# A routed MoE step on one core: the second tile's root, the last bias products and the first block's opening moved within the routing

## The chip, the cores and the metric

The kernel runs on one core of one Trainium2 chip. The metric is the device time of one execution in microseconds (us). The median of three executions stands against the median of the changed kernel. One further execution was profiled.

## The reference, cut to what matters

One trunk layer over 528 prompt rows and 8 sample rows (536 tokens, width 1024): a mixer (diagonal state space and gated convolution), an output projection, and a mixture of experts. Around the change this is computed:

```python
x  = x + mix @ w_out                                  # residual after the mixer
hf = rmsnorm(x, norm_ffn)                             # input of router and experts
logits = hf @ w_router + b_router                     # 32 experts
top_v, top_i = lax.top_k(logits, 4)
gates = softmax(top_v)
# tokens are sorted by expert and laid into blocks of 128 rows, one expert each
gu = xe @ w_gate_up[e] + b_gate_up[e]                 # 1024 -> 2048
gate, up = min(gu[:, :1024], 7), clip(gu[:, 1024:], -7, 7)
h = gate * sigmoid(1.702 * gate) * (up + 1)
y = h @ w_down[e] + b_down[e]                         # 1024 -> 1024
x = x + sum over the 4 experts of gates * y
out = rmsnorm(x, norm_final)
```

All arrays are float32.

## The kernel before, in words

Three stages share one core, each a block of code of its own with a barrier between them: `mixer`, `router` and `experts`. The change lies in `router` (line 1042 on) and in the opening of `experts` (line 1596 on). Each stage writes out one instruction order for each engine by hand: PE (TensorE, matmuls), DVE (VectorE), ACT (ScalarE), POOL (GpSimd) and SP (SyncE, which issues most DMAs). Semaphores join them; `a.wait_ge(s, n)` holds an engine until the count is there, and everything behind it on that engine with it.

**Router.** The 536 tokens are five tiles, worked in the order `TILES` = 4, 0, 1, 2, 3 (the first holds 24 rows). The number q counts them in that order, and Q = 4 is the last. For each tile PE projects the mixer's output (`project`, L1294), DVE adds it to x (`residual`, L1460 and L1462), ACT squares (`square`), DVE forms the variance (L1468), ACT takes the root by a logarithm and an exponential (`root`, L1187 and L1189), and DVE refines it and writes hf (`normed`, L1416 to L1480). PE transposes x (L1307), ACT copies it out (`take_xT`, L1197), and PE computes the logits (`strips` L1322, `logits` L1328). DVE picks four experts (`pick_experts`, L1488 to L1501), ACT exponentiates (`expo`) and spreads the gates (`spread`, L1225), and DVE forms the gates and splits each in three bf16 parts (`gates`, L1517 to L1528). PE counts ranks (L1334, L1338) and DVE takes them (`take_ranks`, L1511 and L1512).

After the last tile, block 0 of the expert loop is prepared. DVE writes one-hot rows, PE selects the tokens of expert 0 (L1378), DVE makes the index `idx_next`, and POOL gathers those rows of hf from DRAM (L1178). Meanwhile PE computes the gate-weighted b_down rows: ten products, two for each tile (`bias_rows`, L1346). Product j takes the strip of 32 array rows number j % 4 and writes a PSUM bank of the list `BD_BANK`. ACT copies each out (`take_bias`, L1230). The tables for overflow blocks (`overflow_tables` on DVE) need counts (L1383), a prefix sum (L1391) and two limit products (L1394, L1395) of PE. At the end PE transposes the gathered rows (L1400). ACT makes the high half of weight unit 0 and of x (`w_hi` L1270, `x_hi` L1273), and DVE makes the low halves (`w_lo` L1550, `x_lo` L1555).

**Experts.** One block per expert, 32 and one overflow block. A block has 24 weight units. ACT makes a unit's high half (L1753), DVE its low half (L1925), and PE multiplies hi x hi, hi x lo and lo x hi (`products`, L1856, six matmuls a unit). The next block's selection (`select`, L1834) comes ahead of unit 8, its gather after it, and its transpositions (L1841) and bias rows (`set_bias`, L1863, four matmuls of K = 3 that open the banks) ahead of unit 20. Only block 0 has its selection and bias rows outside the loop, behind the barrier.

Of the kernel before, what the change touches and what calls it, by code (L numbers as in the profile page):

```python
# [19 lines left out]
ALU = mybir.AluOpType  # L20
ACT = mybir.ActivationFunctionType
AX_X = mybir.AxisListType.X

P = 128
# [16 lines left out]
E = 32  # L41
# [1000 lines left out]
def router(nc, a, scratch, stack, sb, sem, bank, keep, mid, tb):  # L1042

    def buf(name, shape, dt=F32):
# [48 lines left out]
        "sub exp mask rank_psum ranked acc_set gates gate4 bdn_in gT_psum gT bd_psum step act_step pool_step tabs first_psum xg_clear "  # L1093
        "count_psum extra upto_psum passed over_psum".split())}
    hf_stored = [sem("r_hf_stored0"), sem("r_hf_stored1")]
    keep["landed"] = [sem(f"landed{j}") for j in range(LOADS)]
    keep["loop"] = {n: sem("e_" + n) for n in "onehot idx x_in xT_psum x_hi x_lo w_hi w_lo".split()}
    e = keep["loop"]
# [5 lines left out]
    keep["tiles"] = TILES  # L1104
    BD_BANK = [1, 2, 3, 4, 5, 0, 1, 2, 4, 5]
    BD_AFTER = {6: 1, 7: 2, 8: 4, 9: 5}
    RT = 1.0 / math.sqrt(D)
# [74 lines left out]
    def _(act):  # L1182
# [57 lines left out]
        square(1, 1)  # L1240
        take_strips(0)
        expo(0)
        spread(0)
        root(1)
        for q in range(2, NT):
# [20 lines left out]
        nc.scalar.activation(gT[:, Q * P:NT * P], bank[3][:, 0:P], ACT.Copy).then_inc(s["gT"], 1)  # L1266
        for j in range(5, 2 * NT):
            take_bias(j)
        act.wait_ge(keep["landed"][0], 16)
        nc.scalar.activation(tb["w_hi0"][:, 0, :].rearrange("p (u n) -> p u n", u=2), unit0, ACT.Copy).then_inc(e["w_hi"], 1)  # L1270
        for h in range(2):
            act.wait_ge(*((s["gT_psum"], 3), (e["xT_psum"], 1))[h])
            nc.scalar.activation(tb["x_hi"][:, 4 * h:4 * h + 4, :].rearrange("p k t -> p (k t)"), bank[h][:], ACT.Copy).then_inc(e["x_hi"], 1)  # L1273

    @block.tensor
    def _(pe):
# [96 lines left out]
        for j in range(4):  # L1373
            bias_rows(j)
        ranks(Q)
        pe.wait_ge(e["onehot"], 1)
        for i in range(NT):
            last = nc.tensor.matmul(bank[6][:, 200:203], onehot[:, i, :], tb["slotval"][:, i, 0, 0, :], start=(i == 0), stop=(i == NT - 1))  # L1378
        last.then_inc(s["first_psum"], 1)
        for j in range(4, 2 * Q):  # L1380
            bias_rows(j)
        for j in range(NT):
            last = nc.tensor.matmul(bank[7][0:E, NT * E:NT * E + 1], mask_b[:, j, :], ones_b[:, 0:1], start=(j == 0), stop=(j == NT - 1))  # L1383
        last.then_inc(s["count_psum"], 1)
        pe.wait_ge(s["gate4"], NT)
        pe.wait_ge(keep["bd_sb"], 3)
        nc.tensor.transpose(bank[3][:, 0:P], gate4[:, Q].rearrange("p c e -> p (c e)"), ident[:]).then_inc(s["gT_psum"], 1)
        pe.wait_ge(s["gT"], 2)
        bias_rows(2 * Q)
        pe.wait_ge(s["extra"], 1)  # L1390
        nc.tensor.matmul(bank[7][0:E, NT * E + 1:NT * E + 2], tri[0:E, 0:E], extra_b[:], start=True, stop=True).then_inc(s["upto_psum"], 1)  # L1391
        bias_rows(2 * Q + 1)
        pe.wait_ge(s["passed"], 1)
        nc.tensor.matmul(bank[6][:, 256:256 + NB], ones_b[0:E, :], passed[:], start=True, stop=True)  # L1394
        nc.tensor.matmul(bank[6][:, 256 + NB:256 + 2 * NB], extra_b[:].to_broadcast([E, P]), passed[:], start=True, stop=True).then_inc(s["over_psum"], 1)  # L1395
        pe.wait_ge(e["x_in"], 16)
        pe.wait_ge(keep["bd_sb"], 7)
        for h in range(2):
            for k in range(4 * h, 4 * h + 4):
                last = nc.tensor.transpose(bank[h][:, (k % 4) * P:(k % 4 + 1) * P], xg[:, k * P:(k + 1) * P], ident[:])  # L1400
            last.then_inc(s["gT_psum"] if h == 0 else e["xT_psum"], 1)

    @block.vector
    def _(dve):
# [109 lines left out]
        def gates(q):  # L1514
            i = TILES[q]
            dve.wait_ge(s["exp"], q + 1)
            done(v.tensor_tensor(gate[:, i, :], gate[:, i, :], mask_b[:, i, :], ALU.mult))  # L1517
            done(v.tensor_reduce(gsum[:, i:i + 1], gate[:, i, :], AX_X, ALU.add))
            done(v.tensor_scalar(gsum[:, i:i + 1], gsum[:, i:i + 1], 1e-30, None, ALU.max))
            done(v.reciprocal(gsum[:, i:i + 1], gsum[:, i:i + 1]))  # L1520
            v.tensor_scalar(gate[:, i, :], gate[:, i, :], gsum[:, i:i + 1], None, ALU.mult).then_inc(s["gates"], 1)
            dve.wait_ge(s["gates"], q + 1)
            left = gate
            for c in range(3):
                part = slotval[:, i, :, 1, c]
                done(v.tensor_copy(part, left[:, i, :]))
                if c < 2:
                    done(v.tensor_tensor(rest[:, i, :], left[:, i, :], part, ALU.subtract))  # L1528
                    left = rest

        def overflow_tables():

            nth = tb["iota_s"]
            dve.wait_ge(s["count_psum"], 1)
            done(v.tensor_copy(count[:], bank[7][0:E, NT * E:NT * E + 1]))
            done(v.tensor_scalar(tiles_in[:], nth[0:E, 1:NT], float(P), count[:, 0:1], ALU.mult, ALU.is_lt))
            done(v.tensor_reduce(extra[:], tiles_in[:], AX_X, ALU.add))
            v.tensor_copy(extra_b[:], extra[:]).then_inc(s["extra"], 1)
            dve.wait_ge(s["upto_psum"], 1)
            done(v.tensor_tensor(upto[:], bank[7][0:E, NT * E + 1:NT * E + 2], extra[:], ALU.add))  # L1540
            v.tensor_scalar(passed[:], nth[0:E, 0:NB], upto[:, 0:1], -0.5, ALU.subtract, ALU.is_gt).then_inc(s["passed"], 1)
            dve.wait_ge(s["over_psum"], 1)
            ended, before = bank[6][:, 256:256 + NB], bank[6][:, 256 + NB:256 + 2 * NB]
# [8 lines left out]
            for h in range(2):  # L1552
                dve.wait_ge(e["x_hi"], h + 1)
                c = slice(4 * h, 4 * h + 4)
                last = v.tensor_tensor(tb["x_lo"][:, c, :].rearrange("p k t -> p (k t)"), bank[h][:],  # L1555
                                       tb["x_hi"][:, c, :].rearrange("p k t -> p (k t)").bitcast(F32), ALU.subtract)
# [10 lines left out]
        residual(1, 1)  # L1567
        normed(0)
        pick_experts(0)
        gates(0)  # L1570
        take_ranks(0)
        variance(1)
        normed(1)
        for q in range(2, NT):
            residual(q, 0)
            pick_experts(q - 1)
            gates(q - 1)
            take_ranks(q - 1)
            residual(q, 1)
# [16 lines left out]
def experts(nc, a, out, scratch, stack, sb, sem, bank, keep, mid, tb, landed):  # L1596
# [33 lines left out]
    def total(q):  # L1630
# [3 lines left out]
    s = {n: sem("e_" + n) for n in (  # L1634
        "w_used sel_psum sel bias_used clip sig h hT_psum h_hi h_lo "
        "y_sb y_stored y_out y_free curd turns".split())}
# [192 lines left out]
    def _(pe):  # L1829
# [60 lines left out]

        select(0, 0)
        pe.wait_ge(s["x_lo"], 1)
        set_bias(0)
        with pe.Fori(0, E - 1) as e:
# [6 lines left out]
    def _(dve):  # L1901
# [73 lines left out]
        dve.wait_ge(s["sel_psum"], 1)  # L1975
        v.tensor_reduce(sel[:], bank[7][:, 0:6].rearrange("p (a c) -> p a c", a=2), AX_X, ALU.add).then_inc(s["sel"], 1)
        for j in range(1, SLOTS):
# [66 lines left out]
```

## Time and profile before

| quantity | us |
|---|---|
| median of 3 executions (1466.55 to 1467.43) | 1466.92 |
| the profiled execution | 1467.44 |
| its span, from first to last instruction | 1465.5 |
| PE busy | 1419.3 |
| DVE busy | 1320.9 |
| ACT busy | 1031.1 |

The span is counted from the first instruction. Busy time is the time in which an engine ran its own instructions; it overlaps from engine to engine. In the rows further down, L1346 is line 1346 of the kernel, and PEld is the weight load of TensorE, which overlaps its matmuls.

### The profile page before, as it was taken

Reading aid. Unit: us, or ns where it says so; the run is one execution under the profiler, and the core shown is the slowest. Engines: PE = TensorE matmul, PEld = TensorE weight load, DVE = VectorE, ACT = ScalarE, POOL = GpSimd, SP = SyncE. Lnnn points to the kernel's source line nnn. Section 1 sums busy time; section 2 is a strip of 40 time slices with the busy share of each in tenths; the row PEclk is TensorE's granted clock in tenths of the full one; section 3 lists DMA queues with packets and bytes.
Section 4 is the critical chain, followed back from the end, with each engine's and each line's share of the span. In section 5 each row is a group of like instructions: output and inputs, shape, how many; then the busy total and the mean of one; then the engine's idle time right before and its main releaser. Section 6 shows DMA issues by size and latency. Waiting matters only on the chain.

```text
span 1465.5 us, 22683 instructions
## 1 busy us (share of the span) xinstructions
PE 1419.3 (97%) x7043; PEld 1134.9 (77%) x7044; DVE 1320.9 (90%) x1755; ACT 1031.1 (70%) x1244; POOL 142.1 (10%) x151
## 2 busy tenths in 40 slices
PE   6999999899999999999999999999999999999992
PEld 5888844588888888888888888888888888888882
DVE  4887576899999999999999999999999999999994
ACT  4011432788878888888888888888888887888783
POOL 8100020100000000000000001000000010000000
PEclk9999999799999999999999999999999999999996
DMA  9510572799999999999999999998999999999953
GB/s 308 70 34 1 197 281 115 239 403 383 381 382 375 376 377 368 373 373 376 370 373 374 371 375 375 362 357 356 366 378 375 382 382 372 370 375 372 371 223 122
DMA packets 85286, 469.42 MB, mean 320 GB/s; under 512 B 17935, under 2 KB 19207, under 8 KB 68361
## 3 DMA queue, kind: packets, MB, share of 16 engines
q1 hardware_dynamic: 73160, 447.86, 76.3%
q0 software_dynamic: 12096, 21.18, 6.3%
q8 instruction: 17, 0.28, 0.1%
q14 instruction: 13, 0.10, 0.0%
HBM read 457.56 MB, written 27.82 MB: 331 GB/s over the span
## 4 chain that ended last, share of the span: by engine, by line
PE 80%; DMA 1%; DVE 1%; ACT 0%; issue 0%; SPq 0%; POOLq 0%
PE bank L1856 75%; PE bank L1847 2%; PE bank L1841 2%; PE bank L1863 1%; DMA token_sums<-ymix,row_cur 0%; DMA x<-token_sums 0%; PE bank L1834 0%; DVE x L2006 0%; DVE ymix L2006 0%; ACT ymix L1791 0%; ACT ring_lo L1815 0%; SPq L1692 0%; DVE ssf L71 0%; DVE ssf L69 0%; DVE ssf L68 0%
## 5 line engine op out<-in xcount | busy, mean ns | idle before, releaser
L1925 DVE TENSOR_TENSOR w_lo<-ring_lo,w_hi 128x1024 fp32r<-128x1024 f32 x527 | 610.0, 1220 | 22.5 <-ACT w_hi L1753 22.4
L1753 ACT ACTIVATE w_hi<-ring_lo 128x1024 fp32r<-128x1024 f32 x527 | 544.2, 1058 | 84.9 <-PE bank L1856 80.7
L1856 PE MATMUL bank<-w_hi,x_hi 128*128 128x512 f32 x1056 | 332.7, 396 | 0.0
L1856 PE MATMUL bank<-w_lo,x_hi 128*128 128x512 f32 x1056 | 326.6, 391 | 0.0
L1856 PE MATMUL bank<-w_hi,x_lo 128*128 128x512 f32 x1056 | 326.4, 390 | 0.0
L1925 DVE TENSOR_TENSOR w_lo<-w_out,w_hi 128x1024 fp32r<-128x1024 f32 x264 | 311.2, 1221 | 11.8 <-ACT w_hi L1753 11.8
L1753 ACT ACTIVATE w_hi<-w_out 128x1024 fp32r<-128x1024 f32 x264 | 268.3, 1055 | 18.5 <-PE bank L1856 18.5
L1856 PEld LDWEIGHTS bank<-w_lo,x_hi 128*128 128x128 f32 x1056 | 198.9, 188 | 42.1
L1856 PEld LDWEIGHTS bank<-w_hi,x_lo 128*128 128x128 f32 x1056 | 198.8, 188 | 42.0
L1856 PEld LDWEIGHTS bank<-w_hi,x_hi 128*128 128x128 f32 x1056 | 194.0, 189 | 37.0 <-issue 0.4
L1856 PE MATMUL bank<-w_hi,h_hi 128*128 128x512 f32 x528 | 169.9, 403 | 0.0
L1856 PE MATMUL bank<-w_lo,h_hi 128*128 128x512 f32 x528 | 163.6, 391 | 0.0
L1856 PE MATMUL bank<-w_hi,h_lo 128*128 128x512 f32 x528 | 162.9, 390 | 0.0
L1721 POOL DMA_INDIRECT token_sums<-ymix,row_cur x33 | 52.3, 1585 | 740.3 <-ACT ymix L1791 740.3
L1856 PEld LDWEIGHTS bank<-w_lo,h_hi 128*128 128x128 f32 x528 | 99.1, 188 | 21.8
L1856 PEld LDWEIGHTS bank<-w_hi,h_lo 128*128 128x128 f32 x528 | 99.1, 188 | 21.7
L1856 PEld LDWEIGHTS bank<-w_hi,h_hi 128*128 128x128 f32 x528 | 94.1, 188 | 22.9 <-issue 7.2
L1764 ACT ACTIVATE cmix<-bank 128x512 f32<-128x512 f32 x66 | 39.6, 600 | 64.4 <-PE bank L1856 64.4
L530 PE MATMUL bank<-hT,ring_lo 128*128 128x272 f32 x240 | 74.6, 392 | 0.0
L529 PE MATMUL bank<-hT,ring_lo 128*128 128x264 f32 x240 | 73.6, 388 | 0.0
L1768 ACT ACTIVATE h_hi<-bank 128x512 fp32r<-128x512 f32 x66 | 39.5, 599 | 46.1 <-PE bank L1847 46.1
L1714 POOL DMA_INDIRECT ymix<-ffn_in,idx_next x33 | 38.9, 1178 | 334.8 <-DVE idx_next L1914 334.8
(365 smaller groups left out, 1175.4 us busy)
## 6 DMA issues: line engine op xcount, KB each, us to landing
ring_lo<-in_w_gate_up SPq DMA_DIRECT2D x132, 2048.0 KB, 11.7
w_out<-in_w_down SPq DMA_DIRECT2D x132, 1024.0 KB, 13.9
ring_lo<-in_w_in SPq DMA_DIRECT2D x4, 2048.0 KB, 22.2
w_out<-in_w_out SPq DMA_DIRECT2D x2, 2048.0 KB, 9.0
x<-in_x_prompt SPq DMA_DIRECT2D x6, 512.0 KB, 9.7
bias<-bias_rows SPq DMA_DIRECT2D x132, 3.0 KB
token_sums<-x SPq DMA_DIRECT2D x4, 512.0 KB
ffn_in<-hf SPq DMA_DIRECT2D x4, 512.0 KB, 6.6
```

The lines of the kernel that those rows point to most:

```text
L529: nc.tensor.matmul(lo[:, 0:HALF], w_k(ORDER[n], k), hT[:, k, 0:HALF], start=(k == 0), stop=(k == KD - 1))
L530: last = nc.tensor.matmul(hi[:, 0:REST], w_k(ORDER[n], k), hT[:, k, HALF:TOK], start=(k == 0), stop=(k == KD - 1))
L1714: nc.gpsimd.indirect_dma_start(xg, None, scratch["hf"], bass.IndirectOffsetOnAxis(ap=idx_next[:, 0:1].bitcast(U32), axis=0), bounds_check= ...
L1721: nc.gpsimd.indirect_dma_start(scratch["acc"], bass.IndirectOffsetOnAxis(ap=row_cur[:, 0:1].bitcast(U32), axis=0), yo, None, bounds_check= ...
L1753: nc.scalar.activation(high(j), raw(j), ACT.Copy).then_inc(s["w_hi"], 1)
L1764: nc.scalar.activation(g_sb, bank[2 * half][:], ACT.Gelu_apprx_sigmoid).then_inc(s["sig"], 1)
L1768: nc.scalar.activation(h_hi[:, 4 * half:4 * half + 4, :].rearrange("p k t -> p (k t)"), bank[6 + half][:], ACT.Copy).then_inc(s["h_hi"], 1)
L1841: last = nc.tensor.transpose(bank[6 + k // 4][:, (k % 4) * P:(k % 4 + 1) * P], xg[:, k * P:(k + 1) * P], ident[:])
L1847: last = nc.tensor.transpose(bank[6 + half][:, k * P:(k + 1) * P], h_sb[:, k * P:(k + 1) * P], ident[:])
L1856: last = nc.tensor.matmul(bank[b + u][:], v[:, k, :], part(j)[:, u, :], start=(j == 16 and first), stop=(j in (7, 15, UNITS - 1) and part ...
L1863: last = nc.tensor.matmul(bank[b][:], tb["one_b"][32 * c:32 * c + 3, 0:1].to_broadcast([3, P]), tb["bias"][32 * c:32 * c + 3, :], start=Tr ...
L1925: v.tensor_tensor(low(j), raw(j), high(j).bitcast(F32), ALU.subtract).then_inc(s["w_lo"], 1)
```

## The change

1. In the router, tile q = 1 has its variance (DVE) placed behind `normed(0)` and its root (ACT) ahead of `expo(0)`. The split of gates is a function of its own, `gate_parts`.
2. Bias product 8 goes to bank 3, and products 8 and 9 are issued side by side. The counts go to bank 6 and are taken before the one-hot rows; the prefix sum comes before the two products. For the last tile, `gate_parts` comes behind the overflow counts.
3. ACT converts weight unit 0 before it copies out bias products 8 and 9.
4. Block 0's selection (to bank 6) and its bias rows are computed in the router, and its transpositions go to banks 4 and 7.

```diff
@@ semaphores, banks
-        "count_psum extra upto_psum passed over_psum".split())}
+        "count_psum extra upto_psum passed".split())}
-    keep["loop"] = {n: sem("e_" + n) for n in "onehot idx x_in xT_psum x_hi x_lo w_hi w_lo".split()}
+    keep["loop"] = {n: sem("e_" + n) for n in "onehot idx x_in xT_psum x_hi x_lo w_hi w_lo sel_psum bias_used".split()}
-    BD_BANK = [1, 2, 3, 4, 5, 0, 1, 2, 4, 5]
-    BD_AFTER = {6: 1, 7: 2, 8: 4, 9: 5}
+    BD_BANK = [1, 2, 3, 4, 5, 0, 1, 2, 3, 5]
+    BD_AFTER = {6: 1, 7: 2, 9: 5}
+    XT_BANK = (4, 7)
@@ router, scalar
         take_strips(0)
+        root(1)
         expo(0)
         spread(0)
-        root(1)
...
-        for j in range(5, 2 * NT):
+        for j in range(5, 2 * Q):
             take_bias(j)
         act.wait_ge(keep["landed"][0], 16)
         nc.scalar.activation(tb["w_hi0"]..., unit0, ACT.Copy).then_inc(e["w_hi"], 1)
+        for j in range(2 * Q, 2 * NT):
+            take_bias(j)
         for h in range(2):
             act.wait_ge(*((s["gT_psum"], 3), (e["xT_psum"], 1))[h])
-            nc.scalar.activation(tb["x_hi"]..., bank[h][:], ACT.Copy).then_inc(e["x_hi"], 1)
+            nc.scalar.activation(tb["x_hi"]..., bank[XT_BANK[h]][:], ACT.Copy).then_inc(e["x_hi"], 1)
@@ router, tensor
         ranks(Q)
+        for j in range(NT):
+            last = nc.tensor.matmul(bank[6][0:E, 240:241], mask_b[:, j, :], ones_b[:, 0:1], start=(j == 0), stop=(j == NT - 1))
+        last.then_inc(s["count_psum"], 1)
         pe.wait_ge(e["onehot"], 1)
...
         for j in range(4, 2 * Q):
             bias_rows(j)
-        for j in range(NT):
-            last = nc.tensor.matmul(bank[7][0:E, NT * E:NT * E + 1], mask_b[:, j, :], ones_b[:, 0:1], start=(j == 0), stop=(j == NT - 1))
-        last.then_inc(s["count_psum"], 1)
         pe.wait_ge(s["gate4"], NT)
         pe.wait_ge(keep["bd_sb"], 3)
         nc.tensor.transpose(bank[3][:, 0:P], gate4[:, Q]..., ident[:]).then_inc(s["gT_psum"], 1)
-        pe.wait_ge(s["gT"], 2)
-        bias_rows(2 * Q)
         pe.wait_ge(s["extra"], 1)
         nc.tensor.matmul(bank[7][0:E, NT * E + 1:NT * E + 2], tri[0:E, 0:E], extra_b[:], ...).then_inc(s["upto_psum"], 1)
-        bias_rows(2 * Q + 1)
+        pe.wait_ge(s["gT"], 2)
+        for j in range(2 * Q, 2 * NT):
+            bias_rows(j)
         pe.wait_ge(s["passed"], 1)
         nc.tensor.matmul(bank[6][:, 256:256 + NB], ones_b[0:E, :], passed[:], start=True, stop=True)
-        nc.tensor.matmul(bank[6][:, 256 + NB:256 + 2 * NB], ...).then_inc(s["over_psum"], 1)
+        nc.tensor.matmul(bank[6][:, 256 + NB:256 + 2 * NB], ...)
+        for i in range(NT):
+            last = nc.tensor.matmul(bank[6][:, 208:214], onehot[:, i, :], tb["slotval"][:, i, 0, :, :]..., start=(i == 0), stop=(i == NT - 1))
+        last.then_inc(e["sel_psum"], 1)
         pe.wait_ge(e["x_in"], 16)
-        pe.wait_ge(keep["bd_sb"], 7)
         for h in range(2):
             for k in range(4 * h, 4 * h + 4):
-                last = nc.tensor.transpose(bank[h]..., xg[:, k * P:(k + 1) * P], ident[:])
+                last = nc.tensor.transpose(bank[XT_BANK[h]]..., xg[:, k * P:(k + 1) * P], ident[:])
             last.then_inc(s["gT_psum"] if h == 0 else e["xT_psum"], 1)
+        pe.wait_ge(keep["bd_sb"], 9)
+        pe.wait_ge(bias_in, bias_in0 + 64)
+        for c, b in enumerate((0, 2, 1, 3)):
+            last = nc.tensor.matmul(bank[b][:], tb["one_b"][32 * c:32 * c + 3, 0:1].to_broadcast([3, P]),
+                                    tb["bias"][32 * c:32 * c + 3, :], start=True, stop=False)
+        last.then_inc(e["bias_used"], 1)
@@ router, vector
             dve.wait_ge(s["gates"], q + 1)
+
+        def gate_parts(q):
+            i = TILES[q]
             left = gate
             for c in range(3):
...
             v.tensor_copy(extra_b[:], extra[:]).then_inc(s["extra"], 1)
+            gate_parts(Q)
             dve.wait_ge(s["upto_psum"], 1)
...
-            dve.wait_ge(s["over_psum"], 1)
+            dve.wait_ge(e["sel_psum"], 1)
...
         normed(0)
+        variance(1)
         pick_experts(0)
         gates(0)
+        gate_parts(0)
         take_ranks(0)
-        variance(1)
         normed(1)
@@ experts, tensor
-        select(0, 0)
-        pe.wait_ge(s["x_lo"], 1)
-        set_bias(0)
         with pe.Fori(0, E - 1) as e:
@@ experts, vector
         dve.wait_ge(s["sel_psum"], 1)
-        v.tensor_reduce(sel[:], bank[7][:, 0:6]..., AX_X, ALU.add).then_inc(s["sel"], 1)
+        v.tensor_reduce(sel[:], bank[6][:, 208:214]..., AX_X, ALU.add).then_inc(s["sel"], 1)
```

## Rows read from the trace of the kernel before

**Rows 1.** The page, chain that ended last, by engine and line.

```profile
PE bank L1856 75%; PE bank L1847 2%; PE bank L1841 2%; PE bank L1863 1%; DMA token_sums<-ymix,row_cur 0%; DMA x<-token_sums 0%; PE bank L1834 0%; DVE x L2006 0%; DVE ymix L2006 0%; ACT ymix L1791 0%; ACT ring_lo L1815 0%; SPq L1692 0%; DVE ssf L71 0%; DVE ssf L69 0%; DVE ssf L68 0%
```

**Rows 2.** The chain in order of time: start us, us, what.

```profile
272.14 0.28 PE bank L1834 x5
...
272.96 13.87 PE bank L1856 x48
...
305.53 16.54 PE bank L1856 x72
...
340.81 16.54 PE bank L1856 x72
```

**Rows 3.** Windows: stretch, length, busy us by engine, PEclk, DMA, GB/s.

```profile
261.89:278.86 16.97, 13.71 (x48) 8.23 (x45) 11.30 (x27) 12.08 (x19) 5.67 (x6) 0.50 0.70 251
308.18:343.46 35.28, 35.28 (x171) 28.82 (x170) 33.91 (x38) 28.65 (x33) 2.78 (x2) 1.00 0.98 399
```

**Rows 4.** Order of time, DVE, 213 to 215: start, us, what, [idle before].

```profile
213.54 0.21 DVE L1468 TENSOR_SCALAR row<-row 128x1 f32<-128x1 f32 x1
214.25 0.16 DVE L1416 TENSOR_TENSOR row<-row 128x1 f32<-128x1 f32 x1 [0.50 <-ACT row L1189]
```

**Rows 5.** Order of time, ACT and PE, 214 to 216 us.

```profile
214.12 1.06 ACT L1197 ACTIVATE xT<-bank 128x512 f32<-128x512 f32 x2
...
214.85 0.82 PE L1322 MATMUL bank<-xT,w_r 128*32 128x128 f32 x16 [1.33 <-ACT xT L1197]
```

**Rows 6.** Order of time, PE's weight loads, 224 to 226 us.

```profile
224.58 0.86 PEld L1307 LDWEIGHTS bank<-ident,x 128*128 128x128 f32 x8 [0.60 <-DVE x L1462]
```

**Rows 7.** Order of time, PE, 260 to 270 us.

```profile
260.65 0.28 PE L1378 MATMUL bank<-slotval,cmix 128*128 128x3 bf16 x5 [0.89 <-DVE cmix L1504]
260.86 1.23 PE L1346 MATMUL bank<-bdn,gT 32*128 32x512 f32 x8
...
263.60 2.07 PE L1346 MATMUL bank<-bdn,gT 32*128 32x512 f32 x2 [0.37 <-ACT gT L1266]
...
266.33 0.17 PE L1395 MATMUL bank<-passed,extra_b 32*128 32x21 bf16 x1
...
267.71 1.97 PE L1400 MATMUL bank<-ident,ymix 128*128 128x128 f32 x8
```

**Rows 8.** Order of time, DVE, 262 to 272 us.

```profile
262.39 0.22 DVE L1526 CAST slotval<-gate 128x32 bf16<-128x32 f32 x1
...
263.63 0.15 DVE L1535 COPY count<-bank 32x1 f32<-32x1 f32 x1
...
265.82 0.15 DVE L1540 TENSOR_TENSOR upto<-bank,extra 32x1 f32<-32x1 f32 x1 [1.43 <-PE bank L1391]
...
267.86 0.18 DVE L1544 TENSOR_SCALAR over_i<-bank 128x21 int32<-128x21 f32 x1 [1.63 <-PE bank L1395]
...
268.33 0.17 DVE L1548 TENSOR_SCALAR over_i<-over_f 128x21 int32<-128x21 f32 x1
269.39 1.22 DVE L1550 TENSOR_TENSOR w_lo<-ring_lo,w_hi 128x1024 fp32r<-128x1024 f32 x1 [0.89 <-ACT w_hi L1270]
270.53 1.28 DVE L1555 TENSOR_TENSOR x_lo<-bank,x_hi 128x512 fp32r<-128x512 f32 x2
```

**Rows 9.** Order of time, ACT, 263 to 271 us.

```profile
263.44 1.57 ACT L1230 ACTIVATE x<-bank 128x512 f32<-128x512 f32 x3
...
268.31 1.05 ACT L1270 ACTIVATE w_hi<-ring_lo 128x1024 fp32r<-128x1024 f32 x1
269.26 1.07 ACT L1273 ACTIVATE x_hi<-bank 128x512 fp32r<-128x512 f32 x2
```

**Rows 10.** Order of time, SP's queue and DVE's first low halves.

```profile
266.48 2.09 SPq L1028 DMA_DIRECT2D w_out<-in_w_down  x4
...
273.27 3.50 DVE L1925 TENSOR_TENSOR w_lo<-ring_lo,w_hi 128x1024 fp32r<-128x1024 f32 x3 [0.66 <-ACT w_hi L1753]
```

More of the change, by code:

```diff
@@ L1270, in _ @@
         nc.scalar.activation(tb["w_hi0"][:, 0, :].rearrange("p (u n) -> p u n", u=2), unit0, ACT.Copy).then_inc(e["w_hi"], 1)
+        for j in range(2 * Q, 2 * NT):
+            take_bias(j)
         for h in range(2):
             act.wait_ge(*((s["gT_psum"], 3), (e["xT_psum"], 1))[h])
-            nc.scalar.activation(tb["x_hi"][:, 4 * h:4 * h + 4, :].rearrange("p k t -> p (k t)"), bank[h][:], ACT.Copy).then_inc(e["x_hi"], 1)
+            nc.scalar.activation(tb["x_hi"][:, 4 * h:4 * h + 4, :].rearrange("p k t -> p (k t)"), bank[XT_BANK[h]][:], ACT.Copy).then_inc(e["x_hi"], 1)
     @block.tensor
@@ L1387, in _ @@
         nc.tensor.transpose(bank[3][:, 0:P], gate4[:, Q].rearrange("p c e -> p (c e)"), ident[:]).then_inc(s["gT_psum"], 1)
-        pe.wait_ge(s["gT"], 2)
-        bias_rows(2 * Q)
         pe.wait_ge(s["extra"], 1)
         nc.tensor.matmul(bank[7][0:E, NT * E + 1:NT * E + 2], tri[0:E, 0:E], extra_b[:], start=True, stop=True).then_inc(s["upto_psum"], 1)
-        bias_rows(2 * Q + 1)
+        pe.wait_ge(s["gT"], 2)
+        for j in range(2 * Q, 2 * NT):
+            bias_rows(j)
         pe.wait_ge(s["passed"], 1)
         nc.tensor.matmul(bank[6][:, 256:256 + NB], ones_b[0:E, :], passed[:], start=True, stop=True)
-        nc.tensor.matmul(bank[6][:, 256 + NB:256 + 2 * NB], extra_b[:].to_broadcast([E, P]), passed[:], start=True, stop=True).then_inc(s["over_psum"], 1)
+        nc.tensor.matmul(bank[6][:, 256 + NB:256 + 2 * NB], extra_b[:].to_broadcast([E, P]), passed[:], start=True, stop=True)
+        for i in range(NT):
+            last = nc.tensor.matmul(bank[6][:, 208:214], onehot[:, i, :], tb["slotval"][:, i, 0, :, :].rearrange("p b c -> p (b c)"),
+                                    start=(i == 0), stop=(i == NT - 1))
+        last.then_inc(e["sel_psum"], 1)
         pe.wait_ge(e["x_in"], 16)
-        pe.wait_ge(keep["bd_sb"], 7)
         for h in range(2):
             for k in range(4 * h, 4 * h + 4):
-                last = nc.tensor.transpose(bank[h][:, (k % 4) * P:(k % 4 + 1) * P], xg[:, k * P:(k + 1) * P], ident[:])
+                last = nc.tensor.transpose(bank[XT_BANK[h]][:, (k % 4) * P:(k % 4 + 1) * P], xg[:, k * P:(k + 1) * P], ident[:])
             last.then_inc(s["gT_psum"] if h == 0 else e["xT_psum"], 1)
+        pe.wait_ge(keep["bd_sb"], 9)
[4 more added lines that the diff above has]
+        last.then_inc(e["bias_used"], 1)
     @block.vector
@@ L1534, in overflow_tables @@
             dve.wait_ge(s["count_psum"], 1)
-            done(v.tensor_copy(count[:], bank[7][0:E, NT * E:NT * E + 1]))
+            done(v.tensor_copy(count[:], bank[6][0:E, 240:241]))
             done(v.tensor_scalar(tiles_in[:], nth[0:E, 1:NT], float(P), count[:, 0:1], ALU.mult, ALU.is_lt))
@@ L1554, in overflow_tables @@
                 c = slice(4 * h, 4 * h + 4)
-                last = v.tensor_tensor(tb["x_lo"][:, c, :].rearrange("p k t -> p (k t)"), bank[h][:],
+                last = v.tensor_tensor(tb["x_lo"][:, c, :].rearrange("p k t -> p (k t)"), bank[XT_BANK[h]][:],
                                        tb["x_hi"][:, c, :].rearrange("p k t -> p (k t)").bitcast(F32), ALU.subtract)
@@ L1577, in _ @@
             gates(q - 1)
+            gate_parts(q - 1)
             take_ranks(q - 1)
@@ L1634, in experts @@
     s = {n: sem("e_" + n) for n in (
-        "w_used sel_psum sel bias_used clip sig h hT_psum h_hi h_lo "
+        "w_used sel clip sig h hT_psum h_hi h_lo "
         "y_sb y_stored y_out y_free curd turns".split())}
@@ L1975, in _ @@
         dve.wait_ge(s["sel_psum"], 1)
-        v.tensor_reduce(sel[:], bank[7][:, 0:6].rearrange("p (a c) -> p a c", a=2), AX_X, ALU.add).then_inc(s["sel"], 1)
+        v.tensor_reduce(sel[:], bank[6][:, 208:214].rearrange("p (a c) -> p a c", a=2), AX_X, ALU.add).then_inc(s["sel"], 1)
         for j in range(1, SLOTS):
```

## The prediction

> **What bounds the kernel now.** Read first the chain that ended last, as shares [rows 1]: three quarters of the span are one line of products, L1856 of the expert loop. Next the same chain in order of time [rows 2]: block 0's first product runs at 272.96 us, and the products behind the bias rows of the next two blocks begin at 305.53 and 340.81, 35.28 apart. That pace holds for 33 blocks. So the span is what comes before the first product, the blocks, and the end. The diff leaves the body of a block alone; what it can win lies ahead of the first product. Third, the windows [rows 3]: in a whole block PE is busy for all 35.28 us and DVE for 33.91, so PE sets the pace. They also show the granted clock of TensorE: 0.50 (1.2 GHz) from 261.89 to 278.86, and 1.00 (2.4 GHz) after. Last, the order of time on each engine ahead of the loop [rows 4 to 10]. All times below are this trace's.
>
> **The sum is made against the profiled execution**, 1467.44 us with a span of 1465.5, so 1.94 us lie around the span. The median of the runs shown is 1466.92, 0.52 below the profiled one. I take the saving from there.
>
> **Part A, the second tile's root.** DVE writes the second tile's variance (0.21) at 213.54, behind take_ranks(0). It then stands idle 0.50 until ACT has the root, and begins the Newton steps at 214.25 [rows 4]. The variance goes up behind normed(0); its squares stand ahead of tile 0's exponent on ACT, so they are done by then. Every DVE instruction of tile 0 after it comes 0.21 later, the root is ready long before it is wanted, and the idle 0.50 is gone. DVE gains 0.50. On ACT the root no longer waits behind spread(0), so take_xT(1) follows spread(0) at once instead of starting behind the root at 214.12. PE, which stood 1.33 us for it, stands no more [rows 5]. Is it 1.33 or 0.50? The next place where PE meets DVE is the transposition of tile 2 at 224.58, where PE already waits 0.60 for DVE's residual L1462 [rows 6]. DVE comes there 0.50 earlier, so PE waits 1.43 instead and leaves 0.50 earlier. What is late next is DVE. From there to the end of the projections PE has no more such gap in the order of time, so the 0.50 is kept. Bounds: 0, if a later wait takes it, and 1.33, all that PE stood. I take 0.50.
>
> **Part B, from the gather to the last x_lo.** Before: PE waits for the transposed gates until 263.60. Bias row 8 takes 2.07 us (to 265.67), and row 9 starts behind it and ends at about 267.8. DVE gets the overflow limits only then: their product L1395 had ended at 266.50, but DVE's wait for it ends at 267.86, which I read as a signal that comes behind row 9, issued before it [rows 7, 8]. The block's transpositions also start only at 267.71, though the gathered rows had landed: SyncE, which waits for the same landing, went on at 266.48 [rows 10]. ACT converts weight unit 0 at 268.31, DVE follows at 269.39, and x_lo ends at 271.81 [rows 8, 9].
> After, step by step: the counts are taken while PE waits for the one-hot rows, a cover of 0.89 us for five products such as the one-hot ones behind it (0.28), so free; without that cover they would cost their 0.28. DVE copies them right after gates(Q), at 262.39 instead of 263.63, 1.24 earlier; so extra_b, there at 264.39 before (265.82 less the wait of 1.43), is there at 263.15 [rows 8]. Its product comes before the two rows, and gate_parts(Q), those 1.2 us, fills the time in which DVE waited 1.43. The two rows are issued together at 263.60, in different strips of 32 rows of the array. Four such rows took 1.23 us at 2.4 GHz for most of it, where one alone took 2.07 at 1.2 GHz [rows 7]: four in turn could not fit in it. I price the pair at 2.2, one row and a second weight load: done at 265.8. The two limit products (0.2) and the five moved selection products (0.28) bring the signal to 266.35. Queued behind them are the transpositions, which wait for the gather at 266.5 anyhow, and DVE, which waits for nothing else. Transpositions: 266.5 to 268.5 (1.97, as before). ACT has 0.54 per half (1.07 for two): the second x_hi ends at 269.1. DVE's second x_lo, 0.64: 269.7. The other route, over DVE: limits 266.4 to 267.05 (0.64), w_lo of unit 0 to 268.25 (1.22; its w_hi, now taken by ACT right behind take_bias(7), which ends at 265.01, is ready at 266.1 [rows 9]), first x_lo to 268.9, then the wait for ACT. Both meet at 269.7. Against 271.81 this is 2.1 us. The moved bias matmuls (272.96 less 272.14 and 0.28, so 0.54) run on PE from 268.5 to 269.1, beside ACT and DVE; they need take_bias(8), which follows w_hi by 0.6, at 266.7. SyncE's four issues end at 268.57 as before [rows 10]. Bounds: 0.2, if the rows still run in turn, and 2.5.
>
> **Part C, the first block.** The five selection products and four bias matmuls, 272.14 to 272.96, were between the barrier and the first product [rows 2]. Now that product is first. No row shows PE entering its loop with nothing ahead, so I bound it: the gain is 0 if the entry costs as much as they hid, at most 0.8. A stall is nearer to the top end: unit 1's low half comes from DVE at about 274.4 (the first of three from 273.27) [rows 10], 2.3 after the block's start, and at 1.2 GHz unit 0 keeps PE 2.8 (six matmuls at twice the 0.23 of a later block, 16.54 / 72 [rows 2]). So even a product right at the start finds unit 1 ready. I take 0.6.
>
> **Sum:** 0.5 + 2.1 + 0.6 = 3.2 us. Profiled 1467.44 - 3.2 = 1464.2; for the median 1466.92 - 3.2 = **1463.7**. This needs the clock to rise as long after the first product as now (5.90 us, 272.96 to 278.86 [rows 2, 3]), which costs half of it, 2.95, in both kernels. The likeliest case's own range is 1463.0 to 1464.5.
>
> The Trainium skill (TensorE: Matmul & The Clock Gate, Part 1: The HAM clock gate) says that the chip looks at PE's activity on a schedule of its own, not begun by the kernel, and so the point of the rise differs from run to run. The trace has a single rise, so no row here can bear that out. By that rule the rise is not tied to the first product, and the first and third rivals are its two outcomes.
>
> **Rivals.**
> 1. The clock rises at the same moment as now, 278.86, however early products start. Then the 3.2 us are worked at half speed, worth 1.6: 1465.3. For it: one rise only, with nothing to show what it hangs on. Against: PE's work before it comes earlier as a whole. Chance 0.14.
> 2. The rows stay in turn (row 9 behind row 8 till 267.8). Selection 268.3, transpositions to 270.3, x_lo to 271.6: part B is 0.2, the sum 1.3, time 1465.6. Against: the four rows in 1.23 us. Chance 0.10.
> 3. The clock rises sooner, about 3 us after the first product instead of 5.90, since less of PE's time just before is idle: 1.5 more, 1462.2. Chance 0.12.
> 4. Slower: PE catches up with DVE. Without the pause at the block's start it has no lead of split units before it, and if it stays close behind DVE's halves, each block is paced by handovers between PE, ACT and DVE and not by PE alone. DVE is busy 33.91 of 35.28, so 1.4 us of reserve speaks against it. It decides from 3.2 / 33 = 0.10 us a block; at 0.2 a block it costs 6.6, the sum is +3.4, time 1470.3. Chance 0.04.
>
> **Chances.** Forecast 0.60 (1463.7), rivals 0.14, 0.10, 0.12 and 0.04. About 0.2% (2.9 us, 1464.0) is what a measurement of this kernel can tell from no change. Seven in ten of the forecast's own cases lie below 1464.0, with the third rival 0.42 + 0.12 = 0.54, say 0.55; slower 0.05; the rest, 0.40, within. The range takes in rivals 1 to 3: 1461.9 to 1465.8.
>
> **What would show it.** In the trace after: take_xT(1) right behind spread(0) and no idle before the strips' products of tile 1; PE's wait at tile 2's transposition grown to about 1.4; the gather issued about 0.5 earlier; rows 8 and 9 overlapping, both within 2.3 us; DVE's last x_lo some 3.3 us after the gather's landing, where it is 5.4 now; the first L1856-type product about 0.4 us after that, where it is 1.15 now, at about 269.7; blocks 35.28 apart. The forecast is wrong if the rows do not overlap, if PE waits for w_lo in units 1 to 3, if the low clock after the first product lasts 1 us more or less than 5.90, or if the pace of blocks moves.

## The result, and the profile after

The changed kernel takes 1470.37 us (median of 20 runs, 1467.42 to 1473.86) against 1467.70 for the kernel before (20 runs, 1465.72 to 1470.74): ratio 1.0020, 95% interval 1.0014 to 1.0026. It is 2.7 us slower where 3.2 us faster was forecast. The profiled execution took 1471.15 us with a span of 1469.3 (before: 1467.44 and 1465.5), and is the one read here.

The page: span, engines, then the shares of the chain that ended last (columns as in [rows 1]).

```profile
span 1469.3 us, 22682 instructions
PE 1420.1 (97%) x7043; PEld 1135.4 (77%) x7044; DVE 1320.1 (90%) x1755; ACT 1031.4 (70%) x1244; POOL 141.9 (10%) x151
...
PE 77%; DMA 2%; DVE 1%; issue 1%; ACT 0%; SPq 0%; POOLq 0%; DVEq 0%; ACTq 0%
```

The expert loop's products (L1874 now) still carry it, but their engine's share fell from 80% to 77% and a DMA holds 2% of the chain. Its name is the second thing to look at: the same chain in order of time, around the end of block 0 (start, duration, what).

```profile
288.43 0.03 POOLq L1732
288.45 0.76 issue
289.21 15.96 DMA ymix<-ffn_in,idx_next
305.17 0.05 issue
305.22 1.09 PE bank L1859 x8
306.31 0.33 PE bank L1881 x4
306.64 18.14 PE bank L1874 x72
...
343.50 16.54 PE bank L1874 x72
```

Block 0 gathers the token rows of block 1 (L1714 before, L1732 after). In the kernel before, the chain ran through this stretch on PE alone [rows 2]. Now it runs for 15.96 us over the gather, and the 72 products behind it take 18.14 us instead of 16.54.

The start of the loop did move as planned. The order of time on PE, ahead of the loop (start, duration, instruction, idle before it and what ended it), answers to [rows 7]:

```profile
264.48 2.08 PE L1349 MATMUL bank<-bdn,gT 32*128 32x512 f32 x4 [0.32 <-ACT gT L1267]
267.03 1.97 PE L1406 MATMUL bank<-ident,ymix 128*128 128x128 f32 x8 [0.21 <-DMA ymix<-ffn_in,idx_next]
268.93 0.61 PE L1411 MATMUL bank<-bias,one_b 3*128 3x512 bf16 x4
271.01 1.22 PE L1874 MATMUL bank<-w_hi,x_hi 128*128 128x512 f32 x2 [1.46 <-PEq L108]
```

Two bias rows are done in 2.08 us, one row's time before. The bias matmuls of block 0 lie beside the split of its rows, and the first product is at 271.01 where it was at 272.89.

**Where the time went.** Distances between the same instructions in the two traces, in us:

| stretch | before | after | difference |
|---|---|---|---|
| span start to the routing's first load, code that is the same | 191.44 | 192.33 | +0.89 |
| from there to the first product | 81.45 | 78.68 | -2.77 |
| first product to block 2's | 67.92 | 72.49 | +4.57 |

The sum is +2.69. The first line is a difference between runs (189.9 to 192.3 over the traces taken). The second is the change. The third is the body of blocks 0 and 1, which the change does not touch. Block 2's products begin at 343.50, later blocks are 35.28 apart as before, and the rest of the 3.8 us between the spans is in the last stores, about 1.

**The wait.** The same gather in the two kernels, first before, then after: issue on POOL; its first reader, on PE.

```profile
290.71 1.22 POOL L1714 DMA_INDIRECT ymix<-ffn_in,idx_next  x1 [13.54 <-DVE idx_next L1914]
...
304.17 1.03 PE L1841 MATMUL bank<-ident,ymix 128*128 128x128 f32 x8
```

```profile
289.21 1.21 POOL L1732 DMA_INDIRECT ymix<-ffn_in,idx_next  x1 [13.50 <-DVE idx_next L1929]
...
305.22 1.09 PE L1859 MATMUL bank<-ident,ymix 128*128 128x128 f32 x8 [3.05 <-DMA ymix<-ffn_in,idx_next]
```

Before, it landed 11.3 us after its issue, at 302.0, and was wanted at 304.17: a slack of 2.2 us that stood in the trace and that the prediction did not read. After, PE wants it at 302.17, 2.0 us earlier. It is issued 1.5 us earlier and lands 16.0 us after its issue, at 305.2, which is 3.2 us later on the clock of the trace. 2.0 + 3.2 - 2.2 is the 3.05 us that PE stands. Had it kept its 11.3 us, it would have landed at 300.5 and PE would not have waited. Then the clock falls (columns as in [rows 3]):

```profile
289.20:305.20 16.00, 12.96 (x62) 10.39 (x60) 15.29 (x16) 10.36 (x12) 1.21 (x1) 1.00 1.03 396
...
307.00:309.00 2.00, 2.00 (x7) 1.51 (x6) 1.86 (x3) 1.37 (x2) 0.00 (x0) 0.50 0.99 426
309.00:310.00 1.00, 1.00 (x4) 0.81 (x3) 0.64 (x1) 0.81 (x1) 0.00 (x0) 0.50 0.87 369
310.00:312.00 2.00, 2.00 (x10) 1.62 (x9) 1.22 (x1) 1.04 (x2) 0.00 (x0) 0.90 0.95 395
```

The granted clock (the value ahead of the last two) was 1.00 through the stall and 0.50, 1.2 GHz, from 307 to a little past 310. That is the 1.6 us by which the 72 products grew. 3.05 + 1.6 is the +4.57 of the table to 0.1.

**Why it landed later.** Three groups of transfers share the 16 DMA engines here: block 0's four w_down loads (SyncE), the five additions of token rows (POOL, 2.1 MB in all, on the software queue), and block 1's w_gate_up loads (SyncE). The gather stands behind the additions in POOL's queue. The issues before, then after:

```profile
266.48 2.09 SPq L1028 DMA_DIRECT2D w_out<-in_w_down  x4
272.63 4.54 POOL L1732 DMA_DIRECT2D token_sums<-x  x5 [9.14 <-POOLq L108]
284.54 6.90 SPq L1028 DMA_DIRECT2D ring_lo<-in_w_gate_up  x3
```

```profile
267.06 2.04 SPq L1028 DMA_DIRECT2D w_out<-in_w_down  x4
271.17 4.54 POOL L1750 DMA_DIRECT2D token_sums<-x  x5 [6.99 <-POOLq L108]
283.08 9.13 SPq L1028 DMA_DIRECT2D ring_lo<-in_w_gate_up  x4
```

Additions, w_gate_up loads and gather all hang on the loop's start and came 1.5 us earlier. The w_down loads hang on the landing of block 0's own gather, here called gather(0), and came 0.6 later in this run. The additions thus began 4.1 us behind them, not 6.15, and shared more of their time with them. The queues in the 6.5 us ahead of the w_gate_up loads (packets, MB, share of 16 engines), before (278 to 284.5) and after (276.5 to 283):

```profile
q0 software_dynamic: 308, 1.10, 88.2%
q1 hardware_dynamic: 132, 0.39, 17.7%
```

```profile
q0 software_dynamic: 238, 0.84, 66.5%
q1 hardware_dynamic: 236, 0.90, 38.5%
```

From the first addition's issue to the first w_gate_up load's it is 11.9 us in both. In that time 1.15 MB of the additions moved before and 0.89 MB after: a quarter less was done when the next loads came. Their time from issue to landing:

```profile
L1732 POOL DMA_DIRECT2D token_sums<-x x5: 932/1593/2278, 272.6 to 274.9; - x5
...
DMA to landing us min/median/max: 7.4/12.1/20.9
```

```profile
L1750 POOL DMA_DIRECT2D token_sums<-x x5: 932/1598/2278, 271.2 to 273.4; - x5
...
DMA to landing us min/median/max: 6.7/13.3/25.2
```

The first addition is the small one and the landing times grow with the order of issue, so the largest belongs to the last. It landed at 274.9 + 20.9 = 295.8 before and at 273.4 + 25.2 = 298.6 after, and the gather 6.2 and 6.6 us behind it. The same sum in the experiments:

| kernel | additions moved ahead of block 1's loads, MB | last addition landed | gather issued | gather took | landed | PE waited |
|---|---|---|---|---|---|---|
| before | 1.15 | 295.8 | 290.7 | 11.3 | 302.0 | 0 |
| after | 0.89 | 298.6 | 289.2 | 16.0 | 305.2 | 3.05 |
| after, again (e0) | 0.88 | 299.8 | 288.8 | 17.2 | 306.0 | 3.9 |
| before, w_down loads late (e9) | 0.89 | not in the trace | 291.7 | 14.9 | 306.6 | 2.3 |
| before with part A (e5) | 1.11 | 296.6 | 289.7 | 13.1 | 302.8 | 0.7 |
| after, one load early (e8) | 1.22 | 292.5 | 288.4 | 11.0 | 299.4 | 0 |
| before, one load early (e11) | 1.84 | 288.9 | 291.3 | 10.7 | 302.0 | 0 |
| after, no additions (e2) | none | none | 288.8 | 11.5 | 300.3 | 0 |

Beside weight loads the gather lands 6.2 to 6.9 us behind the last addition, or about 11 us behind its own issue, whichever is later. With 1.15 MB or more of the additions moved by the time the loads come, it takes about 11 us; below that it takes longer, by an amount that the megabytes alone do not give (0.88 to 0.89 goes with 14.9, 16.0 and 17.2).

### The profile page after: what moved, and what is told of

The parts are those of the page before. It is cut to its first block, busy times and chain, and to the rows that moved or that the text cites. A ratio compares the mean times of both kernels' runs of the same rounds, so it can differ in the third digit from the quotient of the medians.

```text
span 1469.3 us, 22682 instructions
## 1 busy us (share of the span) xinstructions
PE 1420.1 (97%) x7043; PEld 1135.4 (77%) x7044; DVE 1320.1 (90%) x1755; ACT 1031.4 (70%) x1244; POOL 141.9 (10%) x151
## 4 chain that ended last, share of the span: by engine, by line
PE 77%; DMA 2%; DVE 1%; issue 1%; ACT 0%; SPq 0%; POOLq 0%; DVEq 0%; ACTq 0%
PE bank L1874 73%; PE bank L1859 2%; PE bank L1865 2%; DMA ymix<-ffn_in,idx_next 1%; PE bank L1881 1%; DVE w_lo L1940 1%; DMA x<-token_sums 0%; DMA token_sums<-ymix,row_cur 0%; PE bank L1852 0%; DVE x L2021 0%; DVE ymix L2021 0%; ACT ymix L1809 0%; ACT w_hi L1771 0%; SPq L1710 0%; DVE cmix L1958 0%
## 5 line engine op out<-in xcount | busy, mean ns | idle before, releaser
L1874 PE MATMUL bank<-w_hi,x_hi 128*128 128x512 f32 x1056 | 332.4, 396 | 1.5 <-PEq L108 1.5
L1874 PE MATMUL bank<-w_lo,x_hi 128*128 128x512 f32 x1056 | 326.6, 391 | 0.0
L1874 PE MATMUL bank<-w_hi,x_lo 128*128 128x512 f32 x1056 | 326.4, 390 | 0.0
L1940 DVE TENSOR_TENSOR w_lo<-w_out,w_hi 128x1024 fp32r<-128x1024 f32 x264 | 311.0, 1219 | 11.5 <-ACT w_hi L1771 11.5
L1874 PEld LDWEIGHTS bank<-w_hi,x_lo 128*128 128x128 f32 x1056 | 198.8, 188 | 42.1
L1874 PEld LDWEIGHTS bank<-w_lo,x_hi 128*128 128x128 f32 x1056 | 198.8, 188 | 42.1
L1874 PEld LDWEIGHTS bank<-w_hi,x_hi 128*128 128x128 f32 x1056 | 193.8, 189 | 38.6 <-issue 2.0
L1874 PE MATMUL bank<-w_hi,h_hi 128*128 128x512 f32 x528 | 170.5, 404 | 0.0
L1874 PE MATMUL bank<-w_lo,h_hi 128*128 128x512 f32 x528 | 164.3, 392 | 0.0
L1874 PE MATMUL bank<-w_hi,h_lo 128*128 128x512 f32 x528 | 163.4, 391 | 0.0
L1874 PEld LDWEIGHTS bank<-w_lo,h_hi 128*128 128x128 f32 x528 | 99.6, 189 | 21.9
L1874 PEld LDWEIGHTS bank<-w_hi,h_lo 128*128 128x128 f32 x528 | 99.5, 188 | 21.9
L1874 PEld LDWEIGHTS bank<-w_hi,h_hi 128*128 128x128 f32 x528 | 94.4, 189 | 23.1 <-issue 7.2
L1732 POOL DMA_INDIRECT ymix<-ffn_in,idx_next x33 | 38.7, 1172 | 334.6 <-DVE idx_next L1929 334.6
```

Source lines behind the costliest of these rows:

```text
L1732: nc.gpsimd.indirect_dma_start(xg, None, scratch["hf"], bass.IndirectOffsetOnAxis(ap=idx_next[:, 0:1].bitcast(U32), axis=0), bounds_check= ...
L1874: last = nc.tensor.matmul(bank[b + u][:], v[:, k, :], part(j)[:, u, :], start=(j == 16 and first), stop=(j in (7, 15, UNITS - 1) and part ...
L1940: v.tensor_tensor(low(j), raw(j), high(j).bitcast(F32), ALU.subtract).then_inc(s["w_lo"], 1)
```

## The experiments

For each stands the median, in brackets the lowest and highest time and the number of runs, then the ratio to the kernel before on the same chip with its 95% interval.

**e0, the changed kernel again**, on the chip of e1, e2 and e4.

> The changed kernel once more, for a second trace. In its first trace PE stood 3.1 us at the transpositions of block 0 for the gather of block 1, which took 16.0 us from issue to landing against 11.3 before. Theory (backlog: the bias additions to the token sums stand ahead of that gather in the software queue and now share the DMA engines with block 0's w_down loads): it is late again, over 14 us, and PE waits over 1 us, wherever else the run falls. Rival (chance of one profile): it lands in 11 to 12 us and PE waits nothing. Time about 1470.4 by both.

1472.68 us (1472.04 to 1473.94, 5), ratio 1.0039 (1.0025 to 1.0053). The wait is there again, 3.9 us. The loss is larger here than in the first comparison, 5.0 us against 2.7.

**e1, the gather ahead of the additions** in POOL's program.

```
+        gather(1)
         for q, i in enumerate(keep["tiles"]):
             ...   # the five additions
-        gather(1)
```

> The changed kernel with POOL issuing the gather of block 1 ahead of the five additions, so that nothing stands ahead of it in the software queue. Backlog: the gather lands within 8 us of its issue, PE's wait of 3.1 us and the starved units behind it (4.9 us in all by the traces) are gone, and the time is 1465.5, if the additions do not now hold up block 0's scatter (needed at about 320); if they do, part of the 4.9 comes back in block 1. Rival (the gather is slowed by the w_gate_up loads alone, which start 1.5 us earlier): landing stays at 14 to 16 us and the time at 1470.4.

1477.72 us (1477.36 to 1478.61, 5), ratio 1.0071 (1.0057 to 1.0084). The gather landed in 11.3 us and PE waited nothing for it. But the additions, issued now beside the weight loads, took far longer, and the scatter of block 0's results waits for them (chain of waits):

```profile
292.01 29.28 DMA token_sums<-x
...
322.18 12.35 DMA token_sums<-ymix,row_cur
```

PE then stood 10.3 us for a low half of the weights: on DVE, whose order puts the next row indices (`row_cur`) ahead of it, they waited 13.5 us for the scatter to end. So the place behind the additions is what makes the gather late, and it cannot just be turned round. The expected 1465.5 was missed by 12 us; the expectation had the scatter as a risk, at no more than 4.9.

**e2, the additions left out** (the results lack the gate-weighted b_down rows; everything else is computed). A wait of SyncE for the additions, ahead of the load of the last norm's weights, is for the low halves of block 0 instead.

```
-        for q, i in enumerate(keep["tiles"]):
-            ...   # the five additions, and the waits for them
```

> The changed kernel with the five additions of the weighted b_down rows to the token sums left out (the result lacks those rows). Backlog: the gather lands within 8 us, no wait of PE in blocks 0 and 1, 1465.5 or a little less. Rival (w_gate_up loads alone): 1470.4 and a landing of 14 to 16 us.

1465.03 us (1463.91 to 1466.65, 11), ratio 0.9984 (0.9975 to 0.9993). No wait on PE at block 1, and the time is 2.7 us under that of before. The profiled runs of e0 and e2 are 5.4 us apart, and e0's wait and low clock add up to 5.5. The DMA share in 280 to 285 is 0.29, so the additions were the load there. The gather still took 11.5 us and not the under 8 expected: the weight loads alone make up that floor.

**e4, the additions moved into the routing**, behind gather(0) on POOL.

> The changed kernel with the five additions issued by POOL in the routing, behind the gather of block 0, some 5 us earlier than in the loop's block. Backlog: they are through earlier, the gather of block 1 lands in about 11 us or less and PE does not wait: 1465.5 to 1466.5, the upper end if their traffic makes the gather of block 0 land later. Rival (w_gate_up loads alone): 1470.4.

1479.91 us (1477.45 to 1480.53, 5), ratio 1.0082 (1.0068 to 1.0096). The first product, PE in order of time:

```profile
283.74 1.21 PE L1874 MATMUL bank<-w_hi,x_hi 128*128 128x512 f32 x2 [15.51 <-PEq L108]
```

PE stood 15.51 us at the barrier between the stages, which opened only at 283.3. The last addition landed at about 282.5 (issued at 266.3, at most 16.2 us to landing). That the barrier waited for it is read from these two times; no wait in the code names it. No theory named this cost. The gather took 11.4 us, which fits, but the time says nothing on the rest.

**e7, block 1's loads held until the additions have landed.**

```
+            sp.wait_ge(keep["bd_added"], 16 * NT)
             for j in range(LOADS):
```

> The changed kernel with SP holding block 1's weight loads until the five additions have landed. Nothing shares the DMA engines with them then once block 0's w_down is in, and the gather behind them is in front of the loads. Backlog: the additions are through by about 287, the gather lands in 11 us or less, PE does not wait at 301.7, and the weights, needed from 301.8 on, still come in time: 1465.0 to 1465.5, as with the additions left out (1465.03). Rival (the loads have too little slack): the gather is in time but PE or ACT waits for weights in block 1, 1468 or more.

1467.94 us (1466.23 to 1470.20, 11), ratio 1.0007 (0.9998 to 1.0016): no difference from before can be told. The gather landed in 4.4 us, at 290.8, the shortest of all for block 1: the additions had landed at about 289.0, 1.8 us ahead of it, and the loads were issued only at 289.17. That is 20.9 us behind the first product, against 12.1 in the changed kernel. ACT's conversion of the weights waited 4.7 us for them, and PE 1.4 for the halves. The rival came in, not the 1465.0 to 1465.5 of the theory. The contention can be moved, not removed in this way.

**e8, one of block 0's four w_down loads ahead of SyncE's wait for the gathered rows**, where the DMA engines have room (their share is 0.47 from 259 to 262 in the changed kernel).

```
+        weight_load(sp, a, keep, mid, 0, 4).then_inc(keep["landed"][4], 16)
         sp.wait_ge(e["x_in"], 16)
-        for j in range(4, LOADS):
+        for j in range(5, LOADS):
```

> The changed kernel with the first of block 0's four w_down loads (1 MB) issued before SP's wait for the gather of block 0, into a stretch where the DMA engines are idle. Backlog: 1 MB is 2.5 us at the 400 GB/s of the loads, so the additions and the gather of block 1 come up to 2.5 us earlier and PE's wait of 3.1 to 3.9 us falls to about 1; 1468 to 1469 against 1470.4 to 1472.7. Rival (the landing depends on the order of issues in the loop alone): wait and time unchanged. By both the gather of block 0 may land up to 0.5 us later.

1465.52 us (1464.85 to 1467.13, 11), ratio 0.9989 (0.9980 to 0.9998). Faster than both kernels, narrowly so against the kernel before, and some 3 us better than expected. The transpositions of block 1, PE in order of time:

```profile
300.72 1.03 PE L1860 MATMUL bank<-ident,ymix 128*128 128x128 f32 x8
```

No wait. gather(0) takes 4.5 us where it took 3.9, and PE stands 0.95 for it where it stood 0.21.

**e10, two of the four loads early.**

> The changed kernel with two of the four w_down loads ahead of SP's wait. One was enough to bring the gather of block 1 down to 11.0 us, which no run went below, so the second can win nothing there; 2 MB need 5 us at 400 GB/s and overlap the gather of block 0, which lands later by 0.5 to 2 us and holds the transpositions: 1466 to 1467.5, against 1465.5 with one. Rival (more relief is more gain): under 1465.2.

1468.02 us (1467.20 to 1469.14, 11), ratio 1.0006 (0.9997 to 1.0015). A little above the expected 1466 to 1467.5. Now gather(0) pays (7.2 us to landing), on the path to the first product, while the gather of block 1 takes 11.1 as with one load:

```profile
268.88 1.97 PE L1408 MATMUL bank<-ident,ymix 128*128 128x128 f32 x8 [3.52 <-DMA ymix<-ffn_in,idx_next]
```

**e9, the kernel before with its w_down loads 3.7 us later** (7.8 us behind the issue of gather(0) where it was 4.1), so that loads and additions stand even closer than in the changed kernel. Nothing of the change is in it.

```
-        sp.wait_ge(e["x_in"], 16)
+        sp.wait_ge(e["xT_psum"], 1)
         for j in range(4, LOADS):
```

> The kernel before with one wait of SP changed: block 0's w_down loads start when block 0's transpositions are done (269.7), 3.2 us later than now (266.5); nothing else differs. Backlog: the distance from w_down to the additions shrinks from 6.1 us to about 3, below the 4.1 of the changed kernel, so the stall appears here too: the gather of block 1 lands over 14 us after its issue and PE waits for it, 1469 to 1472 against 1467.7. Rival (the stall comes from PE and the loads running earlier, or from something else in the diff): no wait, 1467.7.

1470.42 us (1468.88 to 1473.54, 11), ratio 1.0023 (1.0014 to 1.0032): the whole loss, in the old kernel. PE in order of time, then the chain:

```profile
306.65 1.10 PE L1841 MATMUL bank<-ident,ymix 128*128 128x128 f32 x8 [2.31 <-DMA ymix<-ffn_in,idx_next]
```

```profile
308.07 18.16 PE bank L1856 x72
```

The loads were issued at 270.76, the additions 2.9 us behind them, the gather took 14.9 us. The wait of 2.31 us brought the same low clock and the same 18.1 us. Not all fits: at 2.9 us the gather took 14.9, at the changed kernel's 4.1 us it took 16.0 and 17.2, so that distance alone does not give the size.

**e11, the kernel before with one load early.**

> The kernel before with the first of block 0's w_down loads issued ahead of SP's wait, as in the run that beat both kernels (1465.52). Backlog theory: the kernel before has no wait for the gather of block 1 at its transpositions, so nothing is there to be won: 1467.2, and the gather of block 1 lands in 11 us. What remains between this and 1465.52 is then the change's own worth. Rival (the early load is a gain by itself, whatever the routing): 1465.5 here too.

1467.92 us (1465.45 to 1468.28, 11), ratio 0.9997 (0.9988 to 1.0006). Where nothing waited, the early load gains nothing, though the last addition landed 6.9 us earlier.

**e5, part A alone** in the kernel before (the root and the variance moved).

> The kernel before with part A alone, the root and variance of the second tile moved up. In the trace of the changed kernel PE's transposition of tile 4 came 0.6 us earlier against the start of the routing. All that follows moves together, w_down, additions and loads too, so by the backlog theory no stall appears: 1467.1 to 1467.2 against 1467.7, too little to tell by the time, but visible in the trace. Rival (any earlier start costs at the gather): over 1468.

1466.86 us (1465.41 to 1468.04, 11), ratio 0.9996 (0.9987 to 1.0005). From the routing's first load to the transposition of tile 4 it takes 61.80 us, 62.40 before: 0.60 gained. No stall was expected, and PE already waits 0.7 us for the gather, which took 13.1. Loads and additions are 6.1 us apart as before, but 1.11 MB of the additions had moved where it was 1.15, and the clock rose about 2.5 us sooner after the first product, so that PE came to the transpositions earlier. How much of this is the edit's and how much the run's is open; it shows how thin the slack of 2.2 us was.

**e12, e8 with block 0's selection and bias rows back behind the barrier** (part C undone).

> The changed kernel with one early w_down load and with block 0's selection and bias rows back behind the barrier. The trace puts 0.44 us between the barrier-to-product distances of the two kernels (1.08 and 0.64 us from the last x_lo), so the first product comes 0.4 later and the time is 1465.9. Rival (the two cost their whole 0.8 us): 1466.3; rival (the clock hides it): 1465.5. The time alone can't tell these apart; the trace shows the distance.

1465.64 us (1464.58 to 1466.77, 11), ratio 0.9989 (0.9980 to 0.9998). In the trace the last x_lo's end is 1.07 us ahead of the first product, 0.65 in e8: 0.42 for part C. The medians, 0.12 apart, cannot tell that.

**e13, e8 with bias rows 8 and 9 in turn** (part B's main piece undone).

```
+        bias_rows(2 * Q)
         pe.wait_ge(s["extra"], 1)
         nc.tensor.matmul(...)   # the overflow limits
-        for j in range(2 * Q, 2 * NT):
-            bias_rows(j)
+        bias_rows(2 * Q + 1)
```

> The changed kernel with one early w_down load, and bias rows 8 and 9 one behind the other again, with the prefix sum between them. In the changed kernel's trace the two together took 2.08 us at 1.2 GHz; in turn they take 4.15. So the selection and the transpositions come 1.9 to 2.1 us later and the first product too: 1467.3 to 1467.6 against 1465.5 with them side by side, as the kernel before (1467.3). Rival (the pair was not what gained; the gather's landing sets the transpositions anyhow): under 1466.3.

1466.78 us (1465.42 to 1468.28, 11), ratio 0.9996 (0.9987 to 1.0005). The rows take 2.07 us and then 2.08 (266.73 to 268.81), and issue of gather(0) to the end of the last x_lo is 9.0 us, where e8 has 7.85 and the changed kernel 7.3. So beside e8, which differs only in this and the place of the prefix sum, the pair is worth 1.15 in the trace, since e8's transpositions wait for gather(0); beside the changed kernel it is 1.7. The medians are 1.3 apart, with intervals that overlap, and 1466.78 lies between what was expected and its rival.

## Why the prediction was wrong

- **Part A, 0.50.** Right. Distance from the routing's start to the transposition of tile 4: 62.40 before, 61.79 after, 0.61. The strips' products of tile 1 run with no wait for the root, and PE waits 0.74 at the transposition of tile 2 where its weights show 1.57; what it met next was DVE, as said.
- **Part B, 2.1.** Right. Issue of gather(0) to the end of the last x_lo: 9.45 before (262.36 to 271.81), 7.31 after (263.05 to 270.36), 2.14. The pair of rows took 2.08, priced 2.2; two rows in different strips cost no more than one (rival 2 is out; e13).
- **Part C, 0.6.** Sized slightly too high: 1.08 to 0.65 us, 0.44 (e12: 0.42).
- **Between A and B** the run lost 0.41: tile 4's transposition to the issue of gather(0) took 8.93 us, 8.52 before, as the clock had fallen at 259.2 where it fell at 261.89 before, and the bias rows from 257.73 on took 2.58 where they took 2.10. In e0 it fell at 259.7, when these rows were done, and the stretch is 8.57. With that the stretch gained 2.77 of 3.2.
- **The clock after the first product, 5.90 in both.** Near, but not a constant. It was 6.0 before, and 5.3 and 6.15 in the two traces of the changed kernel, where it rose at 276.3 and 276.8, earlier than the 278.9 of before. So rival 1, a rise at the same moment as before, did not come, and rival 3, about 3 us, not in these two either. Over the other kernels it was from 2.9 to 6.2 (2.9 in e12, 3.4 in e5, 3.6 in e9, 6.2 in e13). Half of that spread, about 1.6 us, is the time that can hang on it, half of what the change was to gain. The Trainium skill (TensorE: Matmul & The Clock Gate, Part 1: The HAM clock gate) says the chip looks on a schedule of its own, so that the point of the rise varies by half a microsecond either way. The 0.9 between the two traces of one kernel agrees with it; the 3.3 over kernels that differ little is wider.
- **Blocks 35.28 apart.** Right for every later block. PE never paced itself by handovers; rival 4 named 1470.3, near what was measured, but by a mechanism that is not there.
- **The step that failed** is in the first part: "The diff leaves the body of a block alone; what it can win lies ahead of the first product." What it can lose does not. The sum stopped at the first product, put the cost behind it at nothing, and took each later block as bound by PE whatever came in. The second gather had 2.2 us of slack, and its landing depends on when transfers of another engine are issued. It cost 3.05 us of waiting and 1.6 of clock, more than A, B and C together.

What is shown: without the additions the same change is faster by 2.7 us (e2); with one load moved out of the way by 1.7 (e8, its own runs beside it); and the old kernel loses 3.2 when its loads are moved towards the additions (e9). Open is the exact size of the gather's delay: e9 and e0 do not lie on one line, and how the 16 engines divide themselves between the software queue and the loads is not seen in these traces. Also open is why single runs of the changed kernel move between 1467.4 and 1473.9, and why its loss was 2.7 us in one comparison and 5.0 in another; the clock's spread explains part.

## What to carry to other kernels

Where a change pulls a stage forward, list each transfer that hangs on its start, the transfers that do not move with it, and the slack between each landing and its first reader; one with less slack than the change gains is a rival to be priced, with the low clock that follows a stall. A gather in one queue behind bulk additions waits for them, not for itself. And a load moved into a stretch where the DMA engines are half idle can give the gain back, but only as many as the transfer on the path there can bear: one did here, two did not.

## What the runs showed of the hardware

- A gather of 128 rows landed in 3.9 to 4.1 us with nothing else on the DMA engines (gather(0), before, after and e0), in about 11 beside weight loads, and in 13.1 to 17.2 when it stood behind unfinished additions besides.
- The additions, 2.1 MB on the software queue, moved 1.10 MB in 6.5 us at 88% of the engines' time, while weight loads alone moved 2.36 MB in 6.0 us at 99% (before, 271 to 277). Per byte they cost the engines' time about twice over. Beside full weight loads one of them took 29.3 us to land (e1).
- A stall of PE of 2.3 to 3.9 us was followed by a little over 3 us at 1.2 GHz in three traces (e9, after, e0), 1.6 us more for 72 products each time (18.12, 18.14, 18.16 for 16.54). A stall of 0.7 us (e5) was not.
- The barrier between the stages stayed shut while additions issued ahead of it on POOL were still on their way (e4: the last landed at about 282.5, it opened at 283.3, and PE stood 15.51 us).
